# A two-layer decoder trunk on one core: its start in one block, and one weight load before the output product

## What is computed

```
mod  = silu(c) @ ada_w[layer] + ada_b[layer]        # 6 x 1024: shift, scale, gate, twice
h    = rms(x) * norm_mix_g * (1 + scale1) + shift1
x    = x + gate1 * (mixer(h @ w_in) @ w_out)         # SSD, latent attention, block attention
h    = rms(x) * norm_ffn_g * (1 + scale2) + shift2
x    = x + gate2 * experts(h)                        # 16 experts, each token takes 2 of one group
```

## Time and profile before

| | |
|---|---|
| three runs | 1405.8, 1408.68, 1413.34 us; median 1408.68 |
| the profiled execution | 1411.56 us, of which its span is 1409.7 us |
| TensorE busy, weight loads busy | 93%, 74% of the span |
| VectorE, ScalarE, GpSimd busy | 80%, 52%, 17% |
| mean granted TensorE clock | 0.972 |
| moved between memory and core | 365.93 MB, mean 260 GB/s |

### The profile page before, as it was taken

One profiled execution on the slowest core, in us unless ns is written; L12 is line 12 of the kernel. 1 busy time (PEld: TensorE's weight loads), 2 busy tenths in 40 slices (PEclk: granted clock), 3 DMA queues, 4 the chain that ended last, 5 costly groups with the idle time before them and its releaser, 6 DMA issues.

```text
span 1409.7 us, 16989 instructions
## 1 busy us (share of the span) xinstructions
PE 1312.8 (93%) x6515; PEld 1045.8 (74%) x6515; DVE 1130.7 (80%) x1335; ACT 731.6 (52%) x963; POOL 237.3 (17%) x293
## 2 busy tenths in 40 slices
PE   6799988879989999999999998988998999999995
PEld 3677766667878888888877777666777888888883
DVE  3679867875579999999886998475557999999986
ACT  1424334562337777777624343447223877777760
POOL 0100136431011000000030013445101100000002
PEclk9899998999999999999999999899999999999998
DMA  9686621433579999999766583010347999999965
GB/s 358 244 297 216 224 94 61 149 119 121 212 292 360 411 409 409 406 407 411 263 229 209 171 277 124 1 60 1 150 173 286 369 403 408 401 415 406 405 238 194
DMA packets 90147, 365.93 MB, mean 260 GB/s; under 512 B 5785, under 2 KB 10631, under 8 KB 80464
## 3 DMA queue, kind: packets, MB, share of 16 engines
q1 hardware_dynamic: 67584, 298.71, 55.7%
q0 software_dynamic: 14160, 51.43, 9.4%
q10 hardware_dynamic: 8320, 14.68, 3.0%
HBM read 336.18 MB, written 28.61 MB: 259 GB/s over the span
## 4 chain that ended last, share of the span: by engine, by line
PE 76%; DVE 10%; issue 4%; ACT 3%; POOL 2%; DMA 2%; DVEq 0%; ACTq 0%; POOLq 0%
PE ps L953 9%; PE ps L1302 8%; PE ps L1304 8%; PE ps L1303 8%; PE ps L951 6%; PE ps L1330 4%; PE ps L1331 4%; PE ps L1332 4%; PE ps L1224 2%; PE ps L1226 2%; PE ps L1225 2%; PE ps L1288 2%; PE ps L1095 1%; PE ps L1126 1%; PE ps L920 1%
## 5 line engine op out<-in xcount | busy, mean ns | idle before, releaser
L1302 PE MATMUL ps<-mod_rounded,work_rounded 128*128 128x512 f32 x340 | 136.9, 403 | 1.8 <-DVE work_rounded L2345 1.8
L1304 PE MATMUL ps<-mod_rounded,work_rounded 128*128 128x512 f32 x340 | 134.6, 396 | 0.0
L1303 PE MATMUL ps<-ring_rounded,work_rounded 128*128 128x512 f32 x288 | 113.9, 396 | 0.0
L2204 DVE TENSOR_TENSOR ring_rounded<-ring,mod_rounded 128x2048 fp32r<-128x2048 f32 (+1 forms) x54 | 102.8, 1929 | 1.4
L1303 PE MATMUL ps<-work_rounded 128*128 128x512 f32 x256 | 101.0, 395 | 0.0
L2204 DVE TENSOR_TENSOR work_rounded<-work,mod_rounded 128x2048 fp32r<-128x2048 f32 (+1 forms) x48 | 91.3, 1930 | 10.0 <-ACT mod_rounded L1680 8.8
L2587 POOL DMA_INDIRECT work<-ffn_rows,slot_idx x34 | 42.0, 1235 | 302.0 <-PE ps L1288 269.3
L953 PE MATMUL ps<-ring_rounded,actT_rounded 128*128 128x512 f32 (+2 forms) x256 | 91.1, 356 | 0.0
L1680 ACT ACTIVATE mod_rounded<-ring 128x2048 fp32r<-128x2048 f32 (+1 forms) x54 | 85.9, 1626 | 0.0
L1812 DVE SCALAR_TENSOR_TENSOR gain<-ring,csil,gain 128x512 f32<-128x512 f32 x106 | 80.8, 763 | 3.0
L1700 ACT ACTIVATE work_rounded<-ps 128x512 fp32r<-128x512 f32 x68 | 37.0, 596 | 84.5 <-PE ps L1288 84.5
(11 more groups left out here) (367 smaller groups left out, 3600.9 us busy)
## 6 DMA issues: line engine op xcount, KB each, us to landing
ring<-in_moe_w_up SPq DMA_DIRECT2D x18, 2048.0 KB, 10.7
ring<-in_moe_w_gate SPq DMA_DIRECT2D x18, 2048.0 KB, 10.4
ring<-in_moe_w_down SPq DMA_DIRECT2D x18, 2048.0 KB
work<-in_moe_w_up SPq DMA_DIRECT2D x16, 2048.0 KB, 10.8
work<-in_moe_w_down SPq DMA_DIRECT2D x16, 2048.0 KB, 11.5
work<-in_moe_w_gate SPq DMA_DIRECT2D x16, 2048.0 KB, 10.4
ring<-in_ada_w SPq DMA_DIRECT2D x30, 1024.0 KB, 5.3
expert_rows<-work POOLq DMA_DIRECT2D x32, 512.0 KB, 7.8
```

The source lines that it names most:

```text
L1302: pe.matmul(ps[j][:, :], xl, hi, start=k == 0, stop=False)
L1303: pe.matmul(ps[j][:, :], xh, lo, start=False, stop=False)
L1304: mm = pe.matmul(ps[j][:, :], xh, hi, start=False, stop=k == KD - 1)
L2204: v.tensor_tensor(slots_r[3 * odd + j][:, 512 * k0:512 * k1], slots[3 * odd + j][:, 512 * k0:512 * k1], buf.bitcast(F32), ALU.subtract).th ...
```

## The change

The first block and its barrier are gone; its work stands at the head of the second block, and each semaphore that it uses counts on from there (`start`, `ahead`). Inside it:

- SyncE's order is new: `c` and the first 128 columns of the constants, then the modulation block of the first use, its 8 KB of biases as one row, the rest of the constants, the second block, the one-hot table, `rel_bias`, the third block, the gain, the fourth block, the first `w_in`, and `x` in four transfers with a semaphore each.
- The modulation blocks are taken in the order 2, 3, 0, 1 (scale first). A product of a row of ones with the row of biases adds the biases in PSUM. Of the last block TensorE takes five steps and VectorE three. ScalarE copies the two shift blocks out.
- The halves of the first input weights are split apart in time: the first before the first tile's row of h, the second behind it. The store of the bias rows is waited for later, by SyncE, ScalarE and GpSimd, where each needs it.
- `load_expert(4, 1, 1)` goes ahead of the output product's loads, and slot 5 follows slot 2. For that `yL` moves to `work` 8192, one of the split output weights by 192 columns, and two scratch areas to `work` 19456.

```diff
+    def sem(name, count=0, start=0):
...
-        return sem_, n + layer * per_layer[sem_.num]
+        return sem_, ahead[sem_.num] + n + layer * per_layer[sem_.num]
...
-    y_scratch = view(s0 + 768, 256)
+    y_scratch = view(19456, 256)
...
-    yL = view(6816, KD, S, of=work_r)
-    out_hi = [biasm_r[:, :, :].rearrange("p a b -> p (a b)")] + [view(n, 2048, of=work_r) for n in (17600, 12288, 14336)]
+    yL = view(8192, KD, S, of=work_r)
+    out_hi = [biasm_r[:, :, :].rearrange("p a b -> p (a b)")] + [view(n, 2048, of=work_r) for n in (17408, 12288, 14336)]
...
+    START_ADA = (2, 3, 0, 1)
+    start_bias = work[0:1, 18432:20480]
+    SPLIT_K = 5
...
-    nc.all_engine_barrier(sems_to_clear=all_sems)
...
+                sp.dma_start(prow[0:KD, :], A["c"].rearrange("a (k p) -> (a k) p", p=P)).then_inc(modb_ld, 16)
+                sp.dma_start(cst[:, 0:P], cpack[:, 0:P]).then_inc(modb_ld, 16)
+                first_ada(sp, 0)
+                sp.dma_start(start_bias, A["ada_b"][0:1, 0:2 * D]).then_inc(next_b, 16)
+                sp.dma_start(cst[:, P:], cpack[:, P:]).then_inc(slot_ld[2], 16)
+                first_ada(sp, 1)
+                sp.dma_start(one_hot, bucket_oh).then_inc(slot_ld[2], 16)
+                sp.dma_start(sml[0:32, 0:4], A["rel_bias"]).then_inc(gain_ld, 16)
+                first_ada(sp, 2)
+                load_mix_gain(sp, 0)
+                first_ada(sp, 3)
+                load_first_in(sp, 0)
+                for t in range(T):
+                    sp.dma_start(x[:, t, :], A["x"][0, P * t:P * t + P, :]).then_inc(x_ld[t], 16)
...
+                    if L == 0:
+                        sp.wait_ge(rel_st, 16)
                     load_bias(1)
...
+                    sp.wait_ge(*at(L, yc_ps, KD))
+                    load_expert(4, 1, 1)
                     sp.wait_ge(*at(L, *read_by_pe("out", 0)))
                     load_expert(0, 0, 0)
-                    sp.wait_ge(*at(L, wo_ev, 8))
-                    sp.wait_ge(*at(L, xss, 2 * T))
-                    load_expert(4, 1, 1)
-                    load_expert(5, 2, 1)
                     sp.wait_ge(*at(L, *read_by_pe("out", 1)))
                     load_expert(2, 2, 0)
+                    load_expert(5, 2, 1)
...
+                def first_ada_bias(n, bank):
+                    b = START_ADA[n]
+                    pe.matmul(ps[bank][:, :], cst[0:1, C_ONE:C_ONE + P], start_bias[:, 512 * b:512 * b + 512],
+                              start=False, stop=True).then_inc(ada_ps, 1)
...
+                first_ada_block(0, 6, KD)
+                pe.wait_ge(next_b, 16)
+                pe.wait_ge(slot_ld[2], 32)
+                first_ada_bias(0, 6)
+                pe.wait_ge(gain_ld, 16)
+                pe.wait_ge(vch, 1)
+                for h in range(MH):
...
+                first_ada_total(0, 7, KD, opens=True)
+                first_ada_bias(1, 7)
+                first_ada_block(2, 5, KD)
+                first_ada_bias(2, 5)
+                pe.wait_ge(ach, 3)
+                first_ada_block(3, 1, SPLIT_K)
+                first_ada_total(1, 1, 2 * KD - SPLIT_K, opens=False)
+                first_ada_bias(3, 1)
...
+                a.wait_ge(ada_ps, 3)
+                a.activation(mod[:, 0:512], ps[5][:, :], ACT.Copy).then_inc(ach, 1)
+                first_in_hi(a, 16, halves=(0,))
...
+                        if after_w_out and t == 0 and sums(L) == NADA:
+                            a.wait_ge(*at(L, row_st[2], 16))
+                        a.activation(view(19456, D) if after_w_out else square, x[:, t, :], ACT.Square,
...
                         x_squares(t, False)
+                        if L == 0 and t == 0:
+                            a.wait_ge(ada_ps, 4)
+                            a.activation(mod[:, 512:1024], ps[1][:, :], ACT.Copy).then_inc(ach, 1)
+                            first_in_hi(a, 16, halves=(1,))
...
                             v.tensor_tensor(x_scaled, x[:, t, :], g_, ALU.mult).then_inc(g_used, 1)
+                            if L == 0 and t == 0:
+                                first_in_lo(v, 0, 0)
+                                v.wait_ge(ach, 8)
...
+                            if L == 0 and t == 0:
+                                first_in_lo(v, 1, 0)
                             h_low(t)
```

More of the change, by code:

```diff
@@ L124, in trunk @@
     per_layer = {}
-    def sem(name, count=0):
+    ahead = {}
+    def sem(name, count=0, start=0):
         sems.append(ctx.enter_context(nc.semaphore(name)))
         per_layer[sems[-1].num] = count
+        ahead[sems[-1].num] = start
         return sems[-1]
@@ L332, in trunk @@
     par = sem("small_params_loaded", 224)
[L333 to L338, removed]
+    gain_ld = sem("gain_loaded", 16, 16)
+    next_b = sem("next_shift_scale_loaded", 16, 16)
+    next_in0 = sem("next_first_input_weights_loaded", 16, 16)
+    next_g = sem("next_gain_loaded", 16, 16)
+    ada_ld = [sem(f"ada_piece{j}_loaded", (96, 80, 80)[j], 16) for j in range(3)]
+    ada_late_ld = [sem(f"ada_late_piece{j}_loaded", 64, 16 * (1 - j)) for j in range(2)]
     first_ada_ld = ada_ld + ada_late_ld[0:1]
@@ L458, in trunk @@
     x_added = sem("x_added_by_token", 8)
+    x_ld = [sem(f"x_tile{t}_loaded") for t in range(T)]
+    rel_st = sem("bias_by_distance_stored")
     cdn = sem("token_tile_combined", 4)
@@ L483, in trunk, with first_in_hi @@
     first_half = 4 * in_width[IN_ORDER[0]]
-    def first_in_hi(a, loaded):
+    def first_in_hi(a, loaded, halves=(0, 1)):
         a.wait_ge(next_in0, loaded)
-        for half in range(2):
+        for half in halves:
             cols = slice(first_half * half, first_half * (half + 1))
@@ L504, in trunk @@
     bias_rows = view(13312, MH, 640)
[L506 to L578, removed]
-            v.tensor_copy(sml[32:33, 0:4], work[32:33, 12928:12932]).then_inc(vch, 1)
-            v.wait_ge(par, 16)
-            v.tensor_copy(ident16, ident)
-            v.tensor_copy(negt16, negt)
-            v.wait_ge(ach, 1)
-            first_ada_sum(0, 1)
-            v.wait_ge(next_b, 16)
-            first_ada_out(0, 0, 6)
-            first_ada_out(1, 1, 7)
-            first_ada_sum(1, 3)
[L589 to L594, removed]
-        @block.scalar
-        def _(a):
-            a.wait_ge(acc_ps, 1)
-            a.activation(csil[:], ps[5][:, 0:KD], ACT.Silu).then_inc(ach, 1)
-            for h in range(MH):
-                a.wait_ge(acc_ps, h + 2)
-                a.activation(bias_rows[:, h, 0:512], ps[h][:, :], ACT.Copy).then_inc(ach, 1)
-            a.activation(bias_rows[:, :, 512:640], ps[4][:, :].rearrange("p (h n) -> p h n", h=MH), ACT.Copy
-                         ).then_inc(ach, 1)
-            first_in_hi(a, 16)
@@ L1405, in _ @@
             def _(a):
+                a.wait_ge(acc_ps, 1)
+                a.activation(csil[:], ps[5][:, 0:KD], ACT.Silu).then_inc(ach, 1)
+                for h in range(MH):
+                    a.wait_ge(acc_ps, h + 2)
+                    a.activation(bias_rows[:, h, 0:512], ps[h][:, :], ACT.Copy).then_inc(ach, 1)
+                a.activation(bias_rows[:, :, 512:640], ps[4][:, :].rearrange("p (h n) -> p h n", h=MH), ACT.Copy
+                             ).then_inc(ach, 1)
+                a.wait_ge(ada_ps, 3)
+                a.activation(mod[:, 0:512], ps[5][:, :], ACT.Copy).then_inc(ach, 1)
+                first_in_hi(a, 16, halves=(0,))
                 step = Counted(a, ach)
+                step.n = 8
                 def layer(L):
@@ L1872, in mixer_rows @@
                                     added(L - 1, t + 2)
+                            else:
+                                v.wait_ge(x_ld[t], 48 if t == T - 1 else 16)
+                                v.wait_ge(*at(L, g_used, 0))
                             if t:
@@ L2456, in layer @@
                     if L == 0:
+                        g.wait_ge(rel_st, 16)
                         step(g.memset(zeros, 0.0))
```

90 lines of the change are left out of this document (72 added, 18 removed).

## The result

| | before | after |
|---|---|---|
| three runs, as shown ahead of the prediction | 1408.68 us | |
| twenty runs of each, median | 1415.38 us (1405.8 to 1422.99) | 1406.78 us (1397.51 to 1418.5) |
| ratio after / before | | 0.994, 95% interval 0.9923 to 0.9956 |
| the profiled execution | 1411.56 us, mean clock 0.972 | 1397.51 us, mean clock 0.980 |

The kernel is 0.6% faster, 8.6 us between the medians; the interval of the ratio reaches from 6.2 to 10.9 us. The forecast was 8.4 us less, but the forecast time, 1400.3 us with a range to 1406.0, is missed: the kernel before takes 1415.4 us over twenty runs, not the 1408.7 us of its first three. One run after, 1418.5 us at a mean clock of 0.963, lies over 1.5% above the fastest and is left out of the ratio.

What follows compares the result with a forecast made beforehand. TensorE, busy 93% of the span, was taken as the bound, leaving its gaps and low-clock detours to win. Start -2.4 and two gathers -3.0 each made -8.4 us, a median of 1400.3 us, range 1394.5 to 1406.

Steps and rivals of the forecast that it cites:

- The two places: The kernel's start and the way into the expert stage, which the change touches: 2.4 us less, and 3.0 less per layer.
- the base: Whole kernel: differences read from the profiled run (1411.56 us) were added to the median of 1408.68 us.
- (C): At the start: the clock stays high, 5.4 us more saved, 1394.9 us; chance 0.10.
- (D): At the start: one-row products keep the clock at 1.2 GHz, 11.9 us lost against the sum, 1412.2 us; chance 0.05.
- The start: Up to the input projection: earlier transfers and TensorE's new order of modulation work give 2.4 us less.
- the gap at the second tile: At the start: the second tile's turning, 0.35 us late before, would no longer leave a gap.
- chain's end: At the start: TensorE finishes the fourth modulation block's total and bias at 45.7, the step all else waits for.
- Rival (A): At the start: TensorE's eighteen added passes eat the 2.4 us, only the gathers gain, 1402.7 us; chance 0.17.
- The gathers: First token gather of each layer: with idle engines 4.2 us instead of 7.15 and 7.14, 3.0 us less each.
- the fourth load: Way into the expert stage: the load waiting for the stored rows is issued near 384 and through by 390.
- The estimate of 3.2 us for such a gather: First token gathers: a skill-based alternative giving 10.3 us less in all, 1398.4 us; the row's 4.2 us was used instead.
- Rival (E): Whole kernel: loads do not move or their place does not matter, so no change, 1408.7 us; chance 0.02.

Runs made afterwards that it cites:

- the halves: Two runs: the changed kernel with the expert loads in their old order, ratio 0.9984; the kernel before with only the new load order, ratio 0.9970.
- the start alone: The changed kernel with the expert loads in their old order: 1412.4 us, ratio 0.9984 to the kernel before.
- up_late: The changed kernel with the second up weights loaded after the first gather instead of before the output product: 1405.72 us, ratio 0.9931 to the kernel before.
- load_only: The kernel before with only the new order of the expert loads and the buffers moved for it: 1409.39 us, ratio 0.9970.

## Why the prediction was right or wrong

- **The size and the sign**: 8.4 us less forecast, 8.6 us measured between the medians. The two places and their mechanisms are as forecast. That the numbers agree to 0.2 us is luck: the measurement is good to some 2 us, the path in the profile counts 7.6 us and the halves' runs 6.5 us, and the gathers gave less than their term.
- **The step that failed is the base**, in the words "I add the differences to the median". The median was one of three runs that lie 7.5 us apart; twenty runs put it at 1415.38, 6.7 us higher. I made the range from the cases of the change alone, and put nothing in for the base and for a new sample of such runs. 1415.38 less 8.4 would have been 1407.0, against 1406.78 measured.
- **What makes the runs differ** is in the results and was partly in the profile before: over the nineteen runs after that count, time and mean granted clock go together (correlation -0.91, 1.0 us for each 0.001 of the clock), from 1397.51 us at 0.980 to 1411.7 at 0.966. I had seen 0.972 and its low stretches, and priced the clock only in the start, as (C) and (D).
- **The start**: 2.4 us forecast (2.1 at the first product and the gap at the second tile), 2.9 in the profile (2.5 at the first product), 2.3 in the runs of the start alone, about 3 by the estimate at equal clock. Step by step: first block at 9.8 (9.74); chain's end 45.7 (45.5); turning 47.8 (47.55); product 51.4 (50.98). The gap of 0.35 us at the second tile is gone. Within it two terms offset: the first block's passes warmed up sooner (8.66 us for 9.96), the third block's later (9.48 for 8.6). Rivals (C) and (D), a first product 5.4 us earlier or 11.9 us later than the forecast 51.4, did not occur. The clock gave a spread between them: the same start reached its first product anywhere from 50.5 to 54.3 in the six profiles that have it unedited, five of them by 51.7. Rival (A), a start that gains nothing, is what the sixth shows.
- **The gathers**: 3.0 us each forecast, 1.9 and 2.7 in the profile after, 4.2 us for the two in the runs of the loads alone. The mechanism is shown (loads in front of the gather, whenever the removed one is issued); the term was too large. It priced the new gather at the 4.2 us of one row, and twenty such gathers took 4.8 us in the mean. The prediction also had the fourth load issued near 384 in before's time, 379 in after's, as the stored rows "wait behind less"; they took 8.7 us, not less than 8.3, and it was issued at 381.63. Whether that costs the gathers anything is not shown, as above.
- **The estimate of 3.2 us for such a gather**, worked out from the Trainium skill's figures ("DMA: Bandwidth & Descriptors", on the anatomy of one DMA), was lower than any measured here: 4.1 us is the shortest of the gathers looked at, with other transfers nearly absent. The row was the better price, and still a little too good.
- **Rival (E)** and the wait for a slot in the first experts did not occur: the second expert's waits are those of before.

## What to carry to other kernels

When a transfer has no work to hide behind, count the bytes issued in front of it and move any that can wait or go earlier to either side; here it did not matter which side. When a kernel's low-clock stretches move from run to run, make the forecast as a ratio and add the spread of the base to the range, and read two profiles against each other place by place, with the granted clock of each place beside it, before giving their difference to the change. A wait of one or two microseconds between small products can bring the low clock; filling it cured that here, though the runs do not yet show the gain in time.

## What was not expected of the hardware

- A wait of 1.6 us of TensorE ahead of the small products came with up to 10 us at 1.2 GHz, from the wait on or soon behind it, in 16 of 20 stretches. Six products of constants in it left none in four.
- The clock fell from 2.4 to 1.2 GHz among products that followed each other with no gap. In ten of the twelve profiles it fell within the 33-row ones, in the other two (`up_late`, `load_only`) with the full product right behind them, with or without wide one-row products in front. That few rows are the reason was not tried.
- The stores of h, half a megabyte, took 8.7 us behind two loads of 2 MB and 8.3 us behind three. How the engines share between the two queues was not looked into.
